# Two transformer blocks on one core: the 40 identity transposes ahead of two norm fills are taken out

## What is computed

```python
def reference(x, ...):
    x = first_block(x, ...)      # mixer, cross attention, feed forward, final norm
    return second_block(x, ...)

# first_block, its end
    u = rmsnorm(h, norm_ff_g[l]) @ w1[l]
    h = h + jnp.square(jax.nn.relu(u)) @ w2[l]
return rmsnorm(h, final_norm_g)

# second_block, its start, and its way from the mixer to the feed forward
    h = rms_norm(x, norm_mix_pre[l])
    proj = h @ w_in[l]
    ...
    x = x + rms_norm(mix @ w_out[l], norm_mix_post[l])
    h2 = rms_norm(x, norm_ffn_pre[l])
    up = causal_depthwise_conv(h2 @ w_up[l], conv_w[l], conv_b[l])
```

## Time and profile before

| | |
|---|---|
| median of three runs | 931.33 us (931.15 to 932.36) |
| the profiled execution | 930.13 us |
| its span, first to last instruction | 928.4 us |
| mean granted TensorE clock over the span | 0.999 |
| TensorE matmuls | 904.3 us busy, 6412 instructions |
| VectorE, ScalarE, GpSimd | 580.2, 496.3, 98.6 us busy |
| traffic with device memory | 155.71 MB read, 1.05 MB written |

### The profile page before, as it was taken

How to read it: one execution, slowest core, us unless ns; L and a number is a source line. 1 busy time by engine, 2 the same in 40 slices (tenths; PEclk the granted TensorE clock), 3 DMA queues, 4 the chain that set the end, 5 groups by cost and what they waited for, 6 DMA issues and landing times.

```text
span 928.4 us, 15993 instructions
## 1 busy us (share of the span) xinstructions
PE 904.3 (97%) x6412; PEld 833.9 (90%) x6412; DVE 580.2 (62%) x762; ACT 496.3 (53%) x725; POOL 98.6 (11%) x148
## 2 busy tenths in 40 slices
PE   6999999999999999999989999999999999999997
PEld 6998988887987999988879988999999799999885
DVE  4774576654644766644455448867587588888643
ACT  5774645534654655533364446666644476666532
POOL 7202122200001000000030006001000200000000
PEclk9999999999999999999999999999999999999999
DMA  7865533225432666555537554454456476775631
GB/s 249 275 235 183 181 98 129 92 96 176 149 124 93 203 192 209 187 187 205 197 102 227 182 181 137 137 182 159 149 181 201 126 185 192 201 194 184 223 136 45
DMA packets 134802, 157.52 MB, mean 170 GB/s; under 512 B 3751, under 2 KB 113565, under 8 KB 134749
## 3 DMA queue, kind: packets, MB, share of 16 engines
q1 hardware_dynamic: 133085, 151.78, 51.3%
q0 software_dynamic: 1056, 3.93, 1.1%
q10 hardware_dynamic: 608, 1.06, 0.3%
HBM read 155.71 MB, written 1.05 MB: 169 GB/s over the span
## 4 chain that ended last, share of the span: by engine, by line
PE 90%; DVE 4%; ACT 3%; POOL 2%; issue 2%; POOLq 0%; DVEq 0%; ACTq 0%
PE tb L576 17%; PE tb L578 16%; PE tb L577 16%; PE acc L576 11%; PE acc L578 10%; PE acc L577 10%; PE tb L654 2%; ACT junk L1098 1%; PE acc L759 1%; DVE wlo L1494 1%; ACT whi L1071 1%; PE tb L851 0%; PE acc L982 0%; PE tb L833 0%; PE acc L964 0%
## 5 line engine op out<-in xcount | busy, mean ns | idle before, releaser
L1494 DVE TENSOR_TENSOR wlo<-raw,whi 128x2048 fp32r<-128x2048 f32 (+1 forms) x143 | 326.9, 2289 | 235.1 <-ACT whi L1071 234.9
L576 PE MATMUL tb<-xhi,whi 128*128 128x256 f32 x1256 | 349.5, 278 | 0.3
L578 PE MATMUL tb<-xhi,wlo 128*128 128x256 f32 x1256 | 347.0, 276 | 0.0
L577 PE MATMUL tb<-xlo,whi 128*128 128x256 f32 x1256 | 346.9, 276 | 0.0
L1071 ACT ACTIVATE whi<-raw 128x2048 fp32r<-128x2048 f32 (+1 forms) x143 | 272.5, 1911 | 134.4 <-PE acc L578 112.0
L576 PEld LDWEIGHTS tb<-xhi,whi 128*128 128x128 f32 x1256 | 235.8, 188 | 1.5 <-issue 0.8
L577 PEld LDWEIGHTS tb<-xlo,whi 128*128 128x128 f32 x1256 | 235.9, 188 | 0.1
L578 PEld LDWEIGHTS tb<-xhi,wlo 128*128 128x128 f32 x1256 | 235.8, 188 | 0.0
L474 POOL TENSOR_SCALAR rs<-ss 128x1 f32<-128x1 f32 x16 | 7.6, 477 | 405.4 <-ACT junk L1098 405.0
L577 PE MATMUL acc<-wlo,hid_hi 128*128 128x512 f32 x128 | 49.8, 389 | 0.0
L576 PE MATMUL acc<-whi,hid_hi 128*128 128x512 f32 x128 | 49.8, 389 | 0.0
(11 more groups left out here) (330 smaller groups left out, 1404.0 us busy)
## 6 DMA issues: line engine op xcount, KB each, us to landing
raw<-in_w_in SPq DMA_DIRECT2D x42, 1024.0 KB, 5.2
raw<-in_w SPq DMA_DIRECT2D x32, 1024.0 KB, 5.2
raw<-in_w_up SPq DMA_DIRECT2D x44, 512.0 KB, 5.0
raw<-in_w_down SPq DMA_DIRECT2D x22, 512.0 KB, 4.1
raw<-in_w_xkv SPq DMA_DIRECT2D x8, 1024.0 KB, 5.3
raw<-in_w_out SPq DMA_DIRECT2D x8, 1024.0 KB, 4.9
raw<-in_w_mem_kv SPq DMA_DIRECT2D x4, 1024.0 KB, 5.1
raw<-in_w_xq SPq DMA_DIRECT2D x4, 1024.0 KB, 5.1
```

The lines of the kernel that those rows point to most:

```text
L576: pe.matmul(o, a_hi, b_hi, start=start, stop=False)
L577: pe.matmul(o, a_hi, b_lo, start=False, stop=False)
L578: return pe.matmul(o, a_lo, b_hi, start=False, stop=stop)
L1494: dve.tensor_tensor(low(n), raw[:, n % RING, :m], whi[:, n % RING, :m].bitcast(F32), ALU.subtract).then_inc(lo_ready, 1)
```

## The change

The helper `keep_clock` and its two calls are taken out. The waits before and behind the calls stay, and so does everything on the other engines.

```diff
733.00:738.21 5.21, 3.22 (x30) 3.01 (x28) 3.58 (x6) 3.58 (x10) 3.56 (x6) 1.00 0.00 0 -661,11 +661,6 733.00:738.21 5.21, 3.22 (x30) 3.01 (x28) 3.58 (x6) 3.58 (x10) 3.56 (x6) 1.00 0.00 0
                 pe.wait_ge(fil["hi"], g0 + n)
                 pe.wait_ge(fil["lo"], g0 + n)
 
-            def keep_clock(n):
-
-                for _ in range(n):
-                    pe.transpose(tb[:, 3, 0:P], ident[:, :], ident[:, :])
-
             pe.wait_ge(consts_ready, 1)
 
             pe.wait_ge(first_rows_in, 32)
733.00:738.21 5.21, 3.22 (x30) 3.01 (x28) 3.58 (x6) 3.58 (x10) 3.56 (x6) 1.00 0.00 0 -908,7 +903,6 733.00:738.21 5.21, 3.22 (x30) 3.01 (x28) 3.58 (x6) 3.58 (x10) 3.56 (x6) 1.00 0.00 0
                 pe.wait_ge(ffn["lo"], j + 1)
                 row_slab(first["w2"] + j, hid_hi, hid_lo, 2 * j, 32)
             emptied(first["w1"] + 15)
-            keep_clock(12)
             pe.wait_ge(nrm["src"], SRC["x2"] + 4)
             fill_norm("x2", xn)
 
733.00:738.21 5.21, 3.22 (x30) 3.01 (x28) 3.58 (x6) 3.58 (x10) 3.56 (x6) 1.00 0.00 0 -1035,7 +1029,6 733.00:738.21 5.21, 3.22 (x30) 3.01 (x28) 3.58 (x6) 3.58 (x10) 3.56 (x6) 1.00 0.00 0
                 pe.wait_ge(mix["lo"], j + 1)
                 row_slab(first["w3"] + j, yhi, ylo, 2 * j, 8)
             emptied(first["ab"] + 3)
-            keep_clock(28)
             fill_norm("h4", h)
             t_loop("cv", 7, "h4")
             n = first["cv"] + 21
```

## The result

The changed kernel took 932.6 us (median of 18 runs, 931.3 to 933.68), the kernel before 931.22 us (18 runs, 930.14 to 932.51). The ratio is 1.0015, with a 95% interval of 1.0008 to 1.0021: slower by 1.4 us, 0.15%, where the prediction had 933.7 us and 0.26%. The profiled execution of the changed kernel took 933.65 us, nearly the longest of its 18; its span is 931.9 us, its mean granted clock 0.991 against 0.999.

The account below looks back on a forecast made before the run. TensorE's matmuls, busy 97% of the span, were taken as the bound. 0 (work) + 0 (x2) + 2.4 (h4) on 930.13 us gives 932.5, plus 1.20 carried over: 933.7 us, +0.26%, range 930.8 to 935.6.

Parts of the forecast that it names:

- The work was free: At x2 and h4, removing 4.69 us of transposes is worth 0 us, since neither group holds up its fill.
- The rival of a faster chain: Norm's chain at x2 and h4 speeds up by 1.0 us without transposes reading SBUF beside GpSimd: 930.3 us, chance 0.03.
- The clock falls at h4: TensorE idles 5.05 us before the fill h4, so the granted clock falls there; fall at h4 alone, chance 0.50.
- I take +2.40, the one row of the same work: Price of a fall at h4: 32 records take 6.71 us at the kernel's start against 4.31 at h4.
- the prediction's lower bound of 1.3 us: At h4, the clock comes back after one half of the tokens, 16 records at 3.36 us against 2.02.
- For the forecast I take 0: At x2, 3.03 us idle is shorter than the one stretch known to lower the clock, so 0 us.
- the prediction's own signs: Clock slices at 0.50 over 736 to 744 us, 1.00 around 480 us; low slices at 480 us too would refute it.
- So 2 us are safe: With transposes in place, 1.99 us idle at h4 left the clock at 1.00; 3.5 us at the end did not.
- 1.20 us under the median, and I carry this over: The profiled execution, 930.13 us, lies 1.20 us under the median 931.33; added to 932.5 this gives 933.7 us.
- Both clocks fall: Rival: 3.03 us idle at x2 lowers the clock as well as h4, 1.7 us more, 935.4 us; chance 0.14.
- Nothing happens: Rival: the clock doesn't fall in the 5.05 us at h4, or in too few executions: 931.3 us, chance 0.33.
- The variant in which transposes count for nothing: Second way to no change: transposes never counted as activity, so h4 already idled 5.05 us at clock 1.00: 931.3 us.

Follow-up runs that it names:

- the kernel without the 28: The kernel before with only the 28 transposes ahead of the fill h4 taken out, the 12 at x2 kept: 931.81 us, ratio 1.0015.
- Without the 12: The kernel before with only the 12 transposes ahead of the fill x2 taken out, the 28 at h4 kept: 931.85 us, ratio 1.0013.
- h4 covered: The kernel before with 44 transposes instead of 28 at h4, the 12 at x2 kept: 930.28 us, ratio 0.9993.
- the full cover: The kernel before with 25 transposes at x2 and 44 at h4 instead of 12 and 28; three runs: 930.11, 930.21, 930.36 us, ratios 0.9993, 0.9989, 0.9992.
- x2 covered: The kernel before with 25 transposes instead of 12 at x2, the 28 at h4 kept: 930.27 us, ratio 0.9994.
- 1.5 us too much: The kernel before with 35 transposes at x2 and 60 at h4, more than the waits hold: 931.44 us, ratio 1.0005.
- the warm start: The kernel before with 25 and 44 transposes and 15 more at the kernel's start; two runs: 931.20 and 931.36 us, ratios 0.9999 and 1.0004.

## Why the prediction was right, and where not

**The work was free: right.** The fills start 0.14 and 0.15 us behind their diagonals, as before, and 4.69 us of removed work gave nothing. The rival of a faster chain is out: GpSimd's steps at h4 take 0.74 and 0.84 us without the transposes, as with them, and at x2 the diagonal is used 3.27 us behind the last product, no sooner than the 3.03 us of before.

**The clock falls at h4: right.** It does in both profiles of the change and in that of the kernel without the 28, and all 11 executions of the latter are low. All 29 executions of the change are low too, though a mean clock doesn't tell at which place.

**The price of a fall at h4: mis-sized.** Forecast 2.40 us, measured 1.94 for the long fall and 1.3 for the short one. The step "I take +2.40, the one row of the same work" took the kernel's start, where by the pace nearly all 32 records ran at the low clock. In the long fall at h4 the clock falls 1.3 us before the fill starts (738.5 against 739.80 us), and that part of the low stretch costs nothing; in the short one it comes back sooner, as the prediction's lower bound of 1.3 us had it.

**"For the forecast I take 0" at x2: wrong.** Without the 12 the clock fell at x2 in all three profiles, and this costs 0.7 to 0.9 us (short) or 1.75 us (long), bounds 0 and 2.7. By the prediction's own signs, low slices at 480 us meant that it was wrong. The reason given, a gap shorter than the one known to lower it, was no reason. That one gap, 3.5 us at the kernel's end, was a single draw: between the last matmul and the fall lie 2.1 us in the profile with h4 covered (matmul's end 923.14, fall at 925.28 us) and 5.0 us in the first of the full cover (922.71, 927.73). The windows hold the two falls, in this order:

```profile
925.00:926.00 1.00, 0.00 (x0) 0.00 (x0) 0.75 (x2) 0.00 (x0) 0.36 (x1) 0.64 1.01 393
927.00:928.00 1.00, 0.00 (x0) 0.00 (x0) 0.00 (x0) 0.00 (x0) 0.00 (x0) 0.86 0.93 356
```

No length of idle time that these profiles show can be called safe.

**"So 2 us are safe": the step that failed.** It read one profiled execution as the kernel's behaviour. The same code with the same 2.0 us lost the clock in three profiles (h4 without the 12, h4 with x2 covered, and x2 at 1.96 us with h4 covered), and kept it in others (x2 at 1.95 us in the second profile of before). With it fell "1.20 us under the median, and I carry this over": the 1.20 us were falls that most executions of before have and the profiled one had not. Against an execution without any, the change costs 2.5 us (932.66, the median of 29, against 930.17), near the +2.4 of the forecast by two errors that offset each other: one fall too dear, the other left out. Against the median it costs 1.4, because before pays 1.0 already. That the result lies in the forecast's range, 1.1 us below its middle, is therefore in part luck; the odds leaned the wrong way, 0.52 for more than 0.2% slower, and it was 0.15%.

**The rivals.** "Both clocks fall" is what happens in the profile; its price of 935.4 us was too high for the same two reasons. "Nothing happens" is out by the interval 1.0008 to 1.0021, though the effect is below the 0.2% that the text set as its bound. The variant in which transposes count for nothing, and with it the rule of the Trainium skill, "TensorE: Matmul & The Clock Gate", Part 4, that transpose mode isn't counted as busy in the same way, predicted no difference between the change and the full cover. By these runs they differ by 2.5 us, with 11 and 1 low executions of 11 on one chip, and the fill at the start got faster behind 15 transposes. The measurement decides: transposes as this kernel issues them, in float32 where the page's own figures there are for bf16, help to hold the clock, and to raise it. Whether they do so to the same degree as matmuls is not shown.

## What to carry to other kernels

A filler that keeps TensorE's clock up does best here when it lasts until the awaited signal, to within some tenths of a microsecond: with a half to two thirds of the wait covered 76 of 117 executions were low, with 0.2 to 0.5 us left open 4 of 33, and 1.5 us too much cost as much as the falls of before had (931.44 us beside 931.13; 1.0005, interval 0.9995 to 1.0014). One profile can't show such an effect, since each execution falls or doesn't; compare the mean clocks and times of many. And before a profiled execution serves as the base of a sum, see where it stands among the runs: one as short as the quickest of 18 is not the kernel.

## What the runs showed that was not expected

The clock also fell with TensorE idle for 0.29 us only, at 126 us behind small products in the first block's attention, and this cost about 1.6 us (in the second profile of the change the last `w2` product ends at 478.39 us instead of 476.76). The low stretches ahead of the last matmul came in two lengths, 3.4 us (ten) and 6.8 us (two), and nothing between in these profiles. The two long ones began 0.7 and 1.3 us before the fill started; of the short ones at x2 and h4 one began 0.5 us before it, the other six behind its start. And the best kernel of the study, at 0.9989 to 0.9993 of before, does more useless work than before: 25 and 44 transposes for 12 and 28. What is left open is why the clock falls at a place in one execution and not in the next, and why the warm start brings more low executions, 14 of 21, where the full cover alone has 4 of 33.
